# Half of a token gather moved into the first expert's second round, with router weights stationary and x turned back to rows earlier

## What is computed

```python
y, ext = pool_mixer(h, ...)              # four trailing windows, a 256x256 map per group of channels
x = x + gate1 * y
h = rms_norm(x, g) * (1 + scale) + shift
logits = h @ router_w + router_b         # 1024 -> 8 experts
top_v, top_i = lax.top_k(logits, 2)
gates = softmax(top_v)
y = sum over e of combine[..., e] * (silu(h @ wg[e]) * (h @ wu[e])) @ wd[e]     # hidden width 3584
x = x + gate2 * y
```

## Time and profile before

| what | value |
| --- | --- |
| median of 3 runs | 2011.12 us (2007.43 to 2011.98) |
| the profiled execution | 2009.45 us |
| its span, first to last instruction | 2007.6 us |
| PE busy | 1770.9 us, 88% |
| DVE, ACT, POOL busy | 424.8, 241.3, 167.3 us |
| HBM read | 473.13 MB |
| chain of waits | PE 78%, DMA 7%, DVE 5%, POOL 4%, issue 3% |

### The profile page before, as it was taken

How to read it: one execution, slowest core, us unless ns; L and a number is a source line. 1 busy time by engine, 2 the same in 40 slices (tenths; PEclk the granted TensorE clock), 3 DMA queues, 4 the chain that set the end, 5 groups by cost and what they waited for, 6 DMA issues and landing times.

```text
span 2007.6 us, 27180 instructions
## 1 busy us (share of the span) xinstructions
PE 1770.9 (88%) x10676; PEld 1295.1 (65%) x10677; DVE 424.8 (21%) x794; ACT 241.3 (12%) x489; POOL 167.3 (8%) x201
## 2 busy tenths in 40 slices
PE   6999886566789999967889999999999999999874
PEld 3766444555567777745339789788777887778331
DVE  2023435965211111275000000000000000000102
ACT  2022242111110000132000000001000010000101
POOL 4002203562000000040000000000000000000001
PEclk8999597666899999978999999999999999999997
DMA  9762042000745554530898868869999999999995
GB/s 342 269 231 88 2 127 57 1 1 27 249 169 210 210 189 159 190 133 2 315 391 325 304 252 319 302 252 354 363 345 345 346 348 352 343 348 367 367 392 211
DMA packets 235294, 481.64 MB, mean 240 GB/s; under 512 B 16575, under 2 KB 90691, under 8 KB 234803
## 3 DMA queue, kind: packets, MB, share of 16 engines
q1 hardware_dynamic: 229755, 471.92, 65.2%
q0 software_dynamic: 3904, 5.44, 0.9%
q10 hardware_dynamic: 1568, 3.34, 0.5%
HBM read 473.13 MB, written 7.90 MB: 240 GB/s over the span
## 4 chain that ended last, share of the span: by engine, by line
PE 78%; DMA 7%; DVE 5%; POOL 4%; issue 3%; ACT 2%; SPq 2%; ACTq 0%; POOLq 0%; DVEq 0%
PE bank L1108 76%; DMA ring<-in_moe_w_up 4%; POOL ring L2301 2%; DMA ring<-in_ada_w 1%; POOL other L2310 1%; ACT ring L1590 1%; SPq L2423 1%; SPq L2388 0%; DVE wide L1882 0%; DVE wide L1866 0%; PE bank L1241 0%; SPq L2414 0%; DVE wide L2204 0%; PE bank L714 0%; DMA ring<-in_cache_fox_logf 0%
## 5 line engine op out<-in xcount | busy, mean ns | idle before, releaser
L1108 PE MATMUL bank<-wide,ring 128*128 128x144 f32 (+4 forms) x4240 | 695.6, 331 | 16.6 <-DVE wide L1878 9.3
L1108 PEld LDWEIGHTS bank<-wide,ring 128*128 128x128 f32 (+2 forms) x4240 | 616.5, 191 | 100.3 <-issue 34.9
L1108 PE MATMUL bank<-ring 128*64 128x512 f32 (+8 forms) x1748 | 339.3, 519 | 50.6 <-DMA ring<-in_moe_w_up 24.5
L1108 PE MATMUL bank<-other,ring 128*128 128x144 f32 (+3 forms) x2016 | 292.2, 320 | 50.3 <-POOL ring L2301 29.8
L1108 PEld LDWEIGHTS bank<-other,ring 128*128 128x128 f32 (+1 forms) x2016 | 267.8, 194 | 75.3 <-POOL ring L2301 31.4
L1108 PEld LDWEIGHTS bank<-ring 128*64 128x64 f32 (+4 forms) x1748 | 143.1, 158 | 226.2 <-issue 189.2
L1108 PE MATMUL bank<-ring,other 128*64 128x512 f32 x560 | 128.0, 596 | 8.4 <-ACT other L747 8.4
L820 DVE TENSOR_TENSOR other<-other,bank 64x512 f32<-64x512 f32 (+1 forms) x40 | 24.5, 613 | 441.6 <-ACT other L744 441.6
L838 DVE TENSOR_TENSOR other<-other,bank 128x288 f32<-128x288 f32 (+3 forms) x48 | 21.4, 446 | 350.9 <-PE bank L1108 324.4
L2367 POOL TENSOR_TENSOR small<-const 128x1 f32<-128x1 f32 x1 | 0.2, 193 | 1074.7 <-DMA expert_rows<-ring 1074.7
L1108 PEld LDWEIGHTS bank<-ring,other 128*64 128x64 f32 x560 | 38.4, 137 | 75.4 <-issue 64.3
(11 more groups left out here) (353 smaller groups left out, 956.5 us busy)
## 6 DMA issues: line engine op xcount, KB each, us to landing
ring<-in_moe_w_gate SPq DMA_DIRECT2D x32, 2048.0 KB, 8.0
ring<-in_moe_w_up SPq DMA_DIRECT2D x32, 2048.0 KB, 12.7
ring<-in_moe_w_down SPq DMA_DIRECT2D x32, 2048.0 KB, 16.8
ring<-in_ada_w SPq DMA_DIRECT2D x24, 2048.0 KB, 13.7
ring<-in_moe_w_gate SPq DMA_DIRECT2D x32, 1536.0 KB, 11.1
ring<-in_moe_w_up SPq DMA_DIRECT2D x32, 1536.0 KB, 14.8
ring<-in_moe_w_down SPq DMA_DIRECT2D x32, 1536.0 KB, 16.5
ring<-in_w_in SPq DMA_DIRECT2D x5, 2048.0 KB, 12.7
```

Of the source, the lines that this page charges most:

```text
L1108: return pe.matmul(out, lhsT, rhs, start=start, stop=stop, skip_group_check=True)
```

## The change

Four things move or go.

1. `rows_back` turns `xT` back to rows in two halves, one ahead of and one behind `mean_square(3)`; ACT copies the first half between `square_all(3)` and `root(3)`, the second behind `root(3)`. The old transposes behind `rank` are gone.
2. The router weights are stationary: 8 matmuls of 288 moving columns give logits with experts on partitions (`scores`), DVE copies them to `logitT`, and three small transposes bring tokens onto partitions.
3. `moe_gather` makes part 0 only. Part 1 is `gather_rest`, which PE runs at the head of the round with number 1, the first expert's second, through four banks, chunk by chunk; ACT and DVE copy there too. The loop starts when the copies of part 0 are done. DVE's `moe_rows` and the clearing of the accumulators come behind those copies.
4. `heavy_rows`, `rows_copied` and `rows_stored` always use 192 rows (`CAP`), with no second form.

```diff
         def moe_gather(pe, mm):
-            for part in range(2):
...
+            for blk, (_, w) in enumerate(BLK):
+                pe.wait_ge(s("hot_ready"), blk + 1)
+                for c in range(DC):
+                    last = mm(B[c][:, 0:N], htok[0:w, blk, P * c:P * (c + 1)], hot[0:w, 0, blk, :], blk == 0, blk == 2)
...
+        def gather_rest(pe, mm):
+
+            B = banks.tiles
+            pe.wait_ge(*after("moe_act", 5))
+            pe.wait_ge(s("hot_ready"), 6)
+            for c in range(DC):
+                if c >= 4:
+                    pe.wait_ge(s("all_dve" if c % 2 else "all_act"), c // 2 + 3)
                 for blk, (_, w) in enumerate(BLK):
...
+                    last = mm(B[c % 4][:, 0:N], htok[0:w, blk, P * c:P * (c + 1)], hot[0:w, 1, blk, :], blk == 0, blk == 2)
+                last.then_inc(s("gather_mm"), 1)
+            pe.wait_ge(s("all_act"), DC)
+            pe.wait_ge(s("all_dve"), DC)
...
-        def heavy_rows(pe, k, heavy, done):
-
+        def heavy_rows(pe, heavy, done):
+
+            k = CAP
...
                     with act.Fori(0, ROUNDS) as r:
                         first = act.snap(ROUNDS * x + r, min_val=0, max_val=ROUNDS * ITEMS)
+                        with act.If(first == 1):
+                            for dst, src in gathered(act, 1, 0):
+                                act.activation(dst, src, ACT.Copy).then_inc(s("all_act"), 1)
...
                     with act.If(held > 0):
-                        by_kind(act, many, rows_copied)
+                        rows_copied(CAP)
...
             moe_gather(pe, mm)
             for sem in ("all_act", "all_dve"):
-                pe.wait_ge(s(sem), DC)
+                pe.wait_ge(s(sem), DC // 2)
...
                     with pe.Fori(0, ROUNDS) as r:
                         first = pe.snap(ROUNDS * x + r, min_val=0, max_val=ROUNDS * ITEMS)
+                        with pe.If(first == 1):
+                            gather_rest(pe, mm)
                         pe.wait_ge(s("xe_ready"), 2 * i + 2)
...
             moe_hot(dve, do, 1)
-            for part in range(2):
-                for dst, src in gathered(dve, part, 1):
-                    dve.tensor_copy(dst, src).then_inc(s("all_dve"), 1)
-                if part == 0:
-                    moe_rows(dve, do)
-            dve.wait_ge(s("all_act"), DC)
-            dve.wait_ge(s("all_dve"), DC)
+            for dst, src in gathered(dve, 0, 1):
+                dve.tensor_copy(dst, src).then_inc(s("all_dve"), 1)
+            dve.wait_ge(s("all_act"), DC // 2)
+            dve.wait_ge(s("all_dve"), DC // 2)
             for i in range(4):
                 m = dve.memset(banks.tiles[ACC + i][:, :], 0.0)
             m.then_inc(s("acc_zero"), 1)
+            moe_rows(dve, do)
             vector_items(dve)
...
+            def rows_back(half):
+
+                for blk, (t0, w) in enumerate(BLK):
+                    b = banks.open(pe, f"xb{half}{blk}", (s("htok_ready"), 3 * half + blk + 1))
+                    for c in range(4):
+                        pe.wait_ge(s("res"), 2 * DC + 4 * half + c + 1)
+                        last = pe.transpose(b[0:w, P * c:P * (c + 1)], xT[:, 4 * half + c, t0:t0 + w], ident)
+                    last.then_inc(s("ht_mm"), 1)
...
+            rows_back(0)
             mean_square(3)
-
-
+            rows_back(1)
+
+
+            b = banks.open(pe, "scores", once("scores_copied"))
+            for c in range(DC):
+                pe.wait_ge(s("h_ready"), 3 * DC + c + 1)
+                last = mm(b[0:NE, 0:N], routerw[:, c, :], hT[:, c, :], c == 0, c == DC - 1)
+            last.then_inc(once.give("scores_mm"), 1)
+            pe.wait_ge(*once("scores_copied"))
             b = banks.open(pe, "route", (s("logits"), 3))
             for blk, (t0, w) in enumerate(BLK):
-                for c in range(DC):
-                    if blk == 0:
-                        pe.wait_ge(s("h_ready"), 3 * DC + c + 1)
-                    last = mm(b[0:w, NE * blk:NE * (blk + 1)], hT[:, c, t0:t0 + w], routerw[:, c, :], c == 0, c == DC - 1)
+                last = pe.transpose(b[0:w, NE * blk:NE * (blk + 1)], logitT[0:NE, t0:t0 + w], ident[0:NE, 0:NE])
...
             square_all(3)
+            rows_back(0)
             root(3)
...
+            rows_back(1)
...
+            dve.wait_ge(*once("scores_mm"))
+            do(dve.tensor_copy(logitT, banks["scores"][0:NE, 0:N]), once.give("scores_copied"))
             dve.wait_ge(*once("route_mm"))
```

More of the change, by code:

```diff
@@ L505, in build_program @@
         slot_of = R.cut(6, ITEMS)
+        logitT = R.cut(N, rows=NE)
         pairs = R.cut(1)
@@ L866, in vector_items @@
                         first = dve.snap(ROUNDS * x + r, min_val=0, max_val=ROUNDS * ITEMS)
+                        with dve.If(first == 1):
+                            for dst, src in gathered(dve, 1, 1):
+                                dve.tensor_copy(dst, src).then_inc(s("all_dve"), 1)
                         R = dve.snap(first + r * both, min_val=0, max_val=ROUNDS * ITEMS)
@@ L931, in moe_tensor @@
                     with pe.If(held > 0):
-                        by_kind(pe, many, lambda k: heavy_rows(pe, k, heavy, ROUNDS * x + ROUNDS + ROUNDS * both))
+                        heavy_rows(pe, heavy, ROUNDS * x + ROUNDS + ROUNDS * both)
         def gathered(engine, part, odd):
@@ L937, in gathered @@
                 engine.wait_ge(s("gather_mm"), DC * part + c + 1)
-                yield xall[:, c, N * part:N * (part + 1)], banks.tiles[c][:, 0:N]
+                yield xall[:, c, N * part:N * (part + 1)], banks.tiles[c % 4 if part else c][:, 0:N]
         def moe_scalar(act):
@@ L943, in moe_scalar @@
             act.activation(small[:, 46:47], ident[:, 0:1], ACT.Copy).then_inc(s("rows_out"), 32)
-            for part in range(2):
-                for dst, src in gathered(act, part, 0):
-                    act.activation(dst, src, ACT.Copy).then_inc(s("all_act"), 1)
-                if part == 0:
[L948 to L953, removed]
+            for dst, src in gathered(act, 0, 0):
+                act.activation(dst, src, ACT.Copy).then_inc(s("all_act"), 1)
+            act.wait_ge(s("all_act"), DC // 2)
+            act.wait_ge(s("all_dve"), DC // 2)
+            act.wait_ge(*once("planned"))
+            take_tokens(act, 0)
             act.wait_ge(*once("pad_zero"))
@@ L1574, in _ @@
             last.then_inc(once.give("rank_mm"), 1)
[L1575 to L1580, removed]
             moe_tensor(pe, mm)
@@ L1805, in _, with rows_back @@
                 copy(dst[0:w, 512 * (n % 2):512 * (n % 2 + 1)], banks[f"gr{n}"][0:w, :], s("hl_copied"))
+            def rows_back(half):
+                for blk, (_, w) in enumerate(BLK):
+                    act.wait_ge(s("ht_mm"), 3 * half + blk + 1)
+                    copy(xback[0:w, blk, 512 * half:512 * (half + 1)], banks[f"xb{half}{blk}"][0:w, :], s("htok_ready"))
             square_all(3)
+            rows_back(0)
             root(3)
[L1808 to L1812, removed]
+            rows_back(1)
             act.wait_ge(s("pool_stored"), 16 * (2 + NB))
@@ L2360, in _ @@
             pool.wait_ge(s("pool_stored"), 16 * (2 + NB))
-            pool.wait_ge(s("ht_mm"), 6)
+            pool.wait_ge(s("ht_mm"), 12)
             me.step(pool.memset(xall[:, :, 2 * N:], 0.0), once.give("pad_zero"))
```

27 lines of the change are left out of this document (12 added, 15 removed).

## The result

The change makes the kernel slower: 2153.75 us (median of 4 runs, 2152.14 to 2157.52) against 2011.05 of the kernel before beside it, a ratio of 1.0708 (95% interval 1.0689 to 1.0726). The forecast was 2005.9, from 2001.5 to 2014.0. The profiled execution of the changed kernel has a span of 2152.4 us, 144.8 over the 2007.6 of before.

What follows compares the result with a forecast made beforehand. The first expert was taken as paced by DMA, 28.2 us per quarter's weights; starting 12.6 us earlier less a 7.4 us DMA gap made 5.2 us, so 2005.9 us against a median of 2011.12, range 2001.5 to 2014.

Steps and rivals of the forecast that it cites:

- fetch rival: Rounds of the pairs: if the longer loop no longer stays fetched, twelve rounds pay 2.72 us each, giving 2039; chance 0.11.
- the sum: Whole kernel: 12.6 us of earlier start less 7.4 us of DMA gap, so 5.2 us earlier.
- Preamble: Ahead of the loop: Ln 1.5 us later, router matmuls 5.9 us, logits 0.7 later, rank matmuls and gather 0.2 later.
- Head start: Loop start: the first expert's matmuls begin at 940.3 in place of 952.92, 12.6 us earlier.
- Hole: First expert's second quarter: the gather there delays weight requests, leaving DMA without work for 7.4 us (6.0 to 9.0).
- Q1 pays for code too: First expert's second quarter: fetching code beside full DMA queues costs 2.72 us or twice that, giving 2008.6 to 2011; chance 0.14.
- Row copies always long: Heavy experts' row stores: 48 more rows go out beside the next slot's round; counted at nothing.

Runs made afterwards that it cites:

- a_pad128: The changed kernel with 128 idle instructions on TensorE ahead of the expert loop; 2033.17 us, ratio 1.012.
- a_pad64: The changed kernel with 64 idle instructions on TensorE ahead of the expert loop; 2085.75 us, run once.
- b_p12: The kernel before with only the change's parts on the path to the router (`rows_back`, stationary router weights); 2016.06 us, ratio 1.0027.
- a_pad104: The changed kernel with 104 idle instructions on TensorE ahead of the expert loop; 2016.69 us, ratio 1.0036.
- a_acc100: Against a_split99: gather pieces go into the four banks of the heavy sums, all but one wait gone, 100 idle instructions; 2010.04 us, ratio 0.999.
- a_nest108: a_acc100 with TensorE's three tests inside one test for the first slot, 108 idle instructions; 2006.53 us, ratio 0.998.
- a_split99: The changed kernel with the gather's second half in three pieces, in the first expert's second to fourth rounds, 99 idle instructions; 2019.29 us, ratio 1.0056.
- p_nest57: a_nest108 without the two parts on the path to the router, 57 idle instructions; 2003.61 us, ratio 0.9959.
- a_pad256: The changed kernel with 256 idle instructions, one whole block, on TensorE ahead of the expert loop; 2166.12 us, run once.

## Why the prediction was wrong

**The step that failed is the fetch rival's weighing.** The mechanism stood in the text: "If the longer loop no longer stays, each of the 12 rounds of the pairs, which PE paces, pays 2.72: 33 us", with 0.11, and against it that "64 instructions are little"; the sum itself counted it at nothing. Chance and price both failed. The chance was argued from the loop's length, 64 instructions more; the runs show that its place decides: the same loop has eight large stops, or, with 128 instructions ahead of it, none that repeats. Nothing in the forecast looked at where the loop would begin, though the change takes code away ahead of it. Whether the 64 instructions are needed besides stays open, since the old loop, at three other places, had one stop each and no row of them. And the price was that of an issue row when the loop is entered in order, 2.72; measured are 16.8 to 18.0 us, with three packets of code one behind the other beside full DMA queues, and some 2 us of low clock follow. Seven stops at that price and one of 11.37 make 131.5 us, 2.9 of which stood there before, of the 144.8. The trace of before had hinted at it: packets of code came at 948.9 and 1110.8, in its own issue row of 7.85 and just ahead of that of 2.72.

The Trainium skill ("Runtime: NRT & Kernel Launch", "Instruction fetch mechanics") gives TensorE room for 2048 instructions and refills it in blocks of 256, which makes eight of them. On the blocks the runs agree: a shift by 256 restores the stops. On the eight places they agree in part: a rule of eight places, set up on the changed kernel (79 packets from the loop's start on) and a_pad128 (13), gave a_pad64's 40 ahead of its run, but missed others (below). The window of two pages in the same section doesn't fit: the first pair's last three rounds, 884 instructions in their 442 records, repeat without one packet.

**The other steps.**
- *Preamble.* Ln at 892.78 (forecast near 893), scores at 5.34 us (5.9), copies of the first half 1.4 us earlier (0.2 later). Near, but the sum left out the clock of what follows: b_p12 shows the two parts costing some 5 us by themselves (2016.06 for 2011.02), where the sum had 0.2.
- *Head start.* 13.6 us for 12.6: near, by two misses against each other. The copies came 1.6 us earlier than forecast, and from their end (931.02) to the first matmul it took 8.3 us, not 7.7.
- *Hole.* 12.2 for 7.4. The gather took 14.83 us, not 12.0: 0.309 us a record at full clock, where the price, 0.25, was from records of the old loop order; three matmuls, six records, in a row now add to one bank. Whether that is the reason wasn't tried. The steps into the round took 2.4 (2.0), and the first tile came free 8.8 us into the round (7.1), at a clock of 0.66 in 980 to 985. These make 2.8 + 0.4 + 1.7 = 4.9 of the 4.8.
- *The sum*, 5.2 earlier, would thus have been 1.4, and the first pair, which begins ahead of all the large stops, shows 0.4. So the 5.2 would not have come without the stops either.
- *"Q1 pays for code too"* was right in a_pad104: 4.85 for 1.90 behind the gather, and 5.50 a quarter later.
- *Row copies always long.* Nothing in the chain, as forecast.

**Left open:** why a_pad104, a_acc100 and a_nest108 fetch blocks again behind the first piece of the gather (15, 13 and 13 packets where the rule has 9) while a_split99 and p_nest57 don't (10 and 9); and the rule's two misses on the old loop. Of eight numbers that the rule gave ahead of a run two came out, one was off by one packet, and five failed. So it is a guess at the mechanism. That the place decides rests on a_pad128, a_pad256 and a_pad64 and not on the rule.

## What to carry to other kernels

Where a loop is long, as here (one round of its first pair passes 884 instructions), an edit anywhere ahead of it moves it and can cost or save more than the edit is about: compare the instruction queue's packets of the two traces first (here 48 and 114), and shift the loop by idle instructions before judging the edit. The first expert's quarters, which DMA paced, had time to spare only for work that waits for nothing: the same records cost 31.4 us a quarter with the waits around them and 26.4 without. And what is gained by taking work from TensorE just ahead of a long stretch can be lost again in its clock, as in b_p12.

## What was not expected of the hardware

In a stop beside full weight queues the blocks of code, 16.4 KB each, came some 6 us apart and one after the other, though each packet took only 1.1 us. The granted clock at the start of a stretch made 54.86 us or up to 57.86 us of the same 336 records, and with the two places behind it gave back more than half of a head start of 12.8 us.
